# Four experts to a block in the last expert loads, and the modulation computed in three groups

## What is computed

```
mod = silu(c) @ w_ada + b_ada            # 1024 -> 6144, and w_ada_f: 1024 -> 2048
sh1, sc1, ga1, sh2, sc2, ga2 = split(mod);   shf, scf = split(silu(c) @ w_ada_f + b_ada_f)
u  = rmsnorm(h, g1) * (1 + sc1) + sh1
h += ga1 * mixer(u)                      # gated conv + gated linear attention, then w_out
u2 = rmsnorm(h, g2) * (1 + sc2) + sh2
h += ga2 * moe(u2)                       # 32 experts (1024 -> 512 -> 1024), 2 of 32 per token
h  = rmsnorm(h, g_final) * (1 + scf) + shf
out = second_block(h)                    # attention, pooling, state-space mixer, w_o, then a feed-forward with w_up, w_down
```

## Time and profile before

| | us |
|---|---|
| median of 3 runs | 1471.61 (1470.12 to 1472.62) |
| the profiled execution | 1468.99 |
| its span | 1467.2 |

### The profile page before, as it was taken

How to read it: one execution, slowest core, us unless ns; L and a number is a source line. 1 busy time by engine, 2 the same in 40 slices (tenths; PEclk the granted TensorE clock), 3 DMA queues, 4 the chain that set the end, 5 groups by cost and what they waited for, 6 DMA issues and landing times.

```text
span 1467.2 us, 20287 instructions
## 1 busy us (share of the span) xinstructions
PE 1226.6 (84%) x8730; PEld 969.2 (66%) x8730; DVE 672.8 (46%) x1103; ACT 456.0 (31%) x651; POOL 1.9 (0%) x15
## 2 busy tenths in 40 slices
PE   6989989998956657566675689999998989899998
PEld 4779887796423223132231389899997979899986
DVE  2647996553200000000000355356656777668974
ACT  1533333533000000000000343334545553554453
POOL 0000000000000000000000000000000000000000
PEclk8899999999979788798788789899998989999999
DMA  9785641996999999999999566343543335345552
GB/s 333 276 299 191 222 144 42 361 337 240 415 419 419 420 419 421 420 419 420 420 420 419 206 195 190 125 125 113 166 152 122 116 115 174 110 162 174 200 201 87
DMA packets 166151, 374.48 MB, mean 255 GB/s; under 512 B 5782, under 2 KB 118824, under 8 KB 141352
## 3 DMA queue, kind: packets, MB, share of 16 engines
q1 hardware_dynamic: 165888, 369.55, 67.8%
q0 software_dynamic: 144, 3.54, 0.7%
q10 hardware_dynamic: 24, 0.03, 0.0%
HBM read 372.02 MB, written 4.62 MB: 257 GB/s over the span
## 4 chain that ended last, share of the span: by engine, by line
PE 57%; DMA 22%; DVE 11%; SPq 5%; ACT 4%; issue 3%; DVEq 0%; ACTq 0%
PE bank L565 31%; DMA arena<-in_w 11%; DMA above<-in_w 8%; SPq L2485 4%; PE bank L1160 4%; DVE arena L1191 4%; PE bank L847 4%; DVE fine L1183 3%; ACT fine L1955 2%; DVE arena L1183 2%; PE bank L877 2%; PE bank L562 2%; PE bank L593 2%; ACT arena L1955 1%; DMA arena<-in_w_in 1%
## 5 line engine op out<-in xcount | busy, mean ns | idle before, releaser
L565 PE MATMUL bank<-fine 128*128 128x256 f32 x4656 | 587.5, 289 | 27.7 <-DVE fine L1183 17.0
L565 PEld LDWEIGHTS bank<-fine 128*128 128x128 f32 x4656 | 577.0, 196 | 37.2 <-issue 33.6
L1183 DVE TENSOR_TENSOR fine<-arena,fine 128x1024 fp32r<-128x1024 f32 (+2 forms) x263 | 300.4, 1167 | 179.7 <-ACT fine L1955 170.1
L1955 ACT ACTIVATE fine<-arena 128x1024 fp32r<-128x1024 f32 (+2 forms) x279 | 267.0, 984 | 181.6 <-PE bank L565 100.3
L1955 ACT ACTIVATE arena<-bank 128x256 f32<-128x256 f32 (+2 forms) x161 | 73.6, 484 | 566.7 <-PE bank L860 181.0
L847 PE MATMUL bank<-arena 128*32 128x512 f32 x640 | 126.1, 810 | 53.3 <-DMA arena<-in_w 34.0
L1183 DVE TENSOR_TENSOR arena<-arena,bank 128x512 f32<-128x512 f32 x8 | 8.4, 1054 | 290.7 <-PE bank L847 290.7
L847 PE MATMUL bank<-above,arena 128*32 128x512 f32 x384 | 78.9, 747 | 54.7 <-issue 25.0
L1955 ACT ACTIVATE arena<-arena 128x512 f32<-128x512 f32 (+6 forms) x94 | 63.2, 703 | 153.2 <-DVE arena L1183 62.0
L1191 DVE SCALAR_TENSOR_TENSOR arena<-arena 128x256 f32<-128x256 f32 (+3 forms) x262 | 107.6, 481 | 1.1 <-ACT arena L1955 0.8
L847 PEld LDWEIGHTS bank<-arena 128*32 128x32 f32 x640 | 31.3, 142 | 110.5 <-issue 110.4
(11 more groups left out here) (162 smaller groups left out, 775.0 us busy)
## 6 DMA issues: line engine op xcount, KB each, us to landing
arena<-in_w SPq DMA_DIRECT2D x120, 1024.0 KB, 26.9
above<-in_w SPq DMA_DIRECT2D x72, 1024.0 KB, 26.5
arena<-in_w_in SPq DMA_DIRECT2D x62, 1024.0 KB, 5.5
arena<-in_w_ada SPq DMA_DIRECT2D x24, 1024.0 KB, 8.9
arena<-in_ffn_w_up SPq DMA_DIRECT2D x22, 1024.0 KB, 5.1
arena<-in_ffn_w_down SPq DMA_DIRECT2D x11, 1024.0 KB, 5.0
arena<-in_w_ada_f SPq DMA_DIRECT2D x8, 1024.0 KB, 12.7
arena<-in_w_gla_o SPq DMA_DIRECT2D x4, 1024.0 KB, 12.1
```

What stands on the lines that cost most here:

```text
L565: ins = e.matmul(o, w[:, k, j * P:j * P + P], x[:, kt, :], start=start, stop=stop, skip_group_check=True)
L1183: return e.tensor_tensor(o, a, b, f)
L1955: return e.activation(o, i, f, bias=bias, scale=scale)
```

## The change

1. **Modulation in three groups**, `ADA = (0..3, 4..9, 10..15)`. All chunks of a group accumulate in bank 7: chunk i of a group puts its sums in row i of each 32-row tile, because the weight is now a window of a zeroed buffer `cz` in which only column 5 holds silu(c). One copy (`rows_ada(g)`), 4 products (`ada_to_mod(g)`, against 4, 6 or 6 columns of `sel`) and one `mod_of(g)` serve a whole group. 16 copies become 3, 64 turning products 12; the sums stay as many.
2. **Order.** Chunks 0 to 3 are loaded into eight separate buffers, without a wait. Chunks 10 and 11 move into level 4 of the mixer, 12 and 13 take the places of 10 and 11, and 14 and 15 those of 12 and 13. Nothing of the modulation is left behind the mixer's last product but the group's turn in quad 0.
3. **First piece.** `make_first` takes the products with the high input part k-tile by k-tile as ACT delivers them, for both halves, and those with the low part last. This holds for the first piece of q, of q2 and of up. For q, ACT and DVE also interleave the halves of the first weight piece with the input tiles.
4. **Two deeper flushes.** PE makes two more half pieces (`flush(1)`) ahead of its wait for the first decay factors and ahead of the wait for `decay_v["kd"]`.
5. **Last four blocks of the experts** (quad 7, blocks 8 to 11) hold one k-tile of all four experts instead of two of two; each is four DMAs of 512 KB instead of two of 1024 KB, in runs of 4 KB instead of 8 KB. PE takes each block by itself, with 8 products, in place of 16 for two blocks.

```diff
-        ada_slots = [flat(gates)[:, 0:SLOT], flat(gates)[:, SLOT:2 * SLOT], flat(St)[:, 0:SLOT], arena[:, q_at:q_at + SLOT]]
+        ada_slots = [flat(gates)[:, 0:SLOT], flat(gates)[:, SLOT:2 * SLOT], flat(St)[:, 0:SLOT], arena[:, q_at:q_at + SLOT],
+                     flat(v), scr[:, 0:SLOT], scr[:, SLOT:2 * SLOT], arena[:, q_at - SLOT:q_at],
+                     arena[:, early_at + SLOT:early_at + 2 * SLOT]]
...
             if f < 8:
-                return f % 4, ada_slots[f % 4], f - 4 if f >= 4 else None
+                return f, ada_slots[f], None
...
+            def make_first(p, half, bank):
+                name, ph = FACTOR[p.name], int(p.n >= PIECES1)
+                def products(kt, x, both, start=False, stop=False):
+                    parts = [shaped(w[:, 0:4 * p.width], 4, p.width) for w in w_parts[ph][(2 * p.n + kt // 4) % NU]]
+                    for j in range(p.width // P):
+                        for i, w in enumerate(parts[:1 + both]):
+                            ins = e.matmul(bank[:, j * 256:j * 256 + 256], w[:, kt % 4, j * P:j * P + P], x[ph][:, kt, :],
+                                           start=start and i + j == 0, stop=stop, skip_group_check=True)
+                    return ins
+                for kt in range(4 * half, 4 * half + 4):
+                    e.wait_ge(*x_hi_a[name, "tile", kt])
+                    products(kt, x_hi, True, start=kt == 0)
+                if half:
+                    for kt in range(KT):
+                        e.wait_ge(*x_lo_v[name, "tile", kt])
+                        ins = products(kt, x_lo, False, stop=kt == KT - 1)
+                        if kt % 4 == 3:
+                            ins.then_inc(*products_of.up((p.n, kt // 4)))
...
-                        ins = e.matmul(bank[32 * k:32 * k + 32, :], cact[:, kt:kt + 1].to_broadcast([P, 32]), slot[:, k, :],
-                                       start=f % 2 == 0, stop=f % 2 == 1, skip_group_check=True)
+                        ins = e.matmul(banks[7][32 * k:32 * k + 32, :], cz[:, kt, 5 - i:37 - i], slot[:, k, :],
+                                       start=f == 2 * ADA[g][0], stop=f == 2 * ADA[g][-1] + 1, skip_group_check=True)
...
+                    if li == 0:
+                        flush(1)
                     e.wait_ge(*decay_v["k", li])
...
-                if li < 4:
-                    ada_to_mod(6 + li)
+                if li == 3:
+                    ada_to_mod(1)
+                if li == 4:
+                    ada_sums(10)
                 for name in fill[done:done + LEVEL_PIECES[li]]:
                     advance(name, 1)
                 done += LEVEL_PIECES[li]
+                if li == 4:
+                    ada_sums(11)
                 if li == STATES_AT:
                     ke3 = shaped(ke, 4, 256)
+                    flush(1)
                     e.wait_ge(*decay_v["kd"])
...
-            ada_sums(10)
+            ada_sums(12)
             advance("gla_o", 2)
-            ada_sums(11)
-            ada_to_mod(10)
+            ada_sums(13)
             advance("gla_o", 2)
             flush()
-            ada_sums(12)
-            ada_to_mod(11)
+            ada_sums(14)
             advance("w_out", 2)
-            ada_sums(13)
-            ada_to_mod(12)
+            ada_sums(15)
             advance("w_out", 2)
             flush()
             norm(1)
-            ada_sums(14)
-            ada_to_mod(13)
-            ada_sums(15)
...
+                if quad == 7:
+                    for k in range(4):
+                        s, _, n = wide_of(quad, 8 + k)
+                        slot = shaped(wides[s], 4, 1024)
+                        e.wait_ge(*wide_in[s][n])
+                        for c in range(2):
+                            for x in range(4):
+                                ins = e.matmul(ob[c][32 * x:32 * x + 32, :], hidT[:, i, k, 32 * x:32 * x + 32],
+                                               slot[:, x, 512 * c:512 * c + 512], start=k == 0, stop=k == 3, skip_group_check=True)
+                        ins.then_inc(*down_made.up((quad, k)))
...
+            scale(0)
+            scale(1)
+            low_half()
+            scale(2)
+            scale(3)
+            low_half()
+            scale(4)
+            scale(5)
+            for k in range(4):
+                rest(k)
+            scale(6)
+            scale(7)
+            for k in range(4, KT):
+                rest(k)
...
+                if quad == 7 and i >= 8:
+                    for x in range(4):
+                        e.dma_start(shaped(wides[s], 4, 1024)[:, x, :], w2v[quad, :, x, i - 8, :]).then_inc(*wide_in[s].up(n, 16))
+                    return
...
-            load("gates", 8)
+            load("gates", 2)
             ada(10)
+            load("gates", 2)
+            ada(11)
+            load("gates", 4)
+            ada(12)
             load("pw", 2)
```

202 lines of the change are left out of this document (99 added, 103 removed).

## The result

| | before | after |
|---|---|---|
| median | 1470.86 (1469.76 to 1472.62) | 1444.75 (1444.07 to 1449.60, 4 runs) |
| the profiled execution | 1468.99 | 1444.07 |
| its span | 1467.2 | 1442.2 |

The same kernel measured once more, on another chip beside nine runs of before, gave 1447.95 against 1471.70, ratio 0.9854 [0.9833, 0.9876]; that time lies in the range. Between its two profiled executions the gain is 24.9 us (1468.99 to 1444.07), and this is the number that the rows can account for. Each kernel has one profiled execution, so a row that depends on the granted clock can differ in the next one; where a second profile tells, it is named.

What follows compares the result with a forecast made beforehand. Bound: PE, DVE and loads in turns through the first mixer, DMA over the experts, then PE. 15.4 + 2 - 0.3 + 2.2 = 19.3 us takes the profiled 1468.99 to 1449.7 and the median 1471.61 to 1452.3; range 1446 to 1461.

Steps and rivals of the forecast that it cites:

- part of it at half clock: At the start: PE's products of q's first piece run from 36.7 to about 47.0 us, partly at half clock.
- Part 1: The start: loads back to back and first input tile earlier, first piece ends sooner; gain 4.1 us, bounds 1.5 and 5.
- which takes about 2 back: Ahead of the experts: rows after some 5 us of PE idling run at half clock, taking back about 2 us.
- Part 5: Mixer's end to experts: PE reaches up products sooner, gain 2.2 us (0.5 to 4.2); block 8 issued 15.4 us earlier.
- Part 2: Up to the decay masks: fewer turns, idling filled, scores at full clock; PE 14.0 us ahead at about 105 us.
- Part 3: The mixer's seven levels: about 14.4 us where DVE becomes the bound, outputs 11 us earlier, bounds 7 and 14.
- rival (a): In the mixer: DVE eats PE's gain through waits for splits; total gain 9 to 14 us, about 1460; chance 0.22.
- Part 4: gla_o and w_out: the 7.53 us modulation wait stays, the turns behind it shrink; gain 2.2 us.
- Part 6: Behind the experts' last byte: 8 products instead of 16 gain 2 us (-1 to +4); shorter rows cost 0.3.
- Rival (d): Stream's end: each 512 KB DMA costs its own 4.5 us landing time; 33 us slower, 1504; chance 0.04.
- Part 7: Block two: first products of q2 and up no longer wait for the first low input tile; gain 2.2 us (1 to 3).
- Rival (b): Level 6 without idling (+3), router (+2) and last burst (+2) at full clock; gain 24 to 27, about 1446; chance 0.10.

Runs made afterwards that it cites:

- hold_scaled: The changed kernel with the loads of expert blocks 3 to 6 also waiting for the normalized input; one execution, 1458.13 us.
- before_again: The kernel before, unchanged, run once more for a second profile; 1470.13 us.
- no_level0_flush: The changed kernel without the flush of two half pieces ahead of the wait for the first decay factors; 1454.69 us, ratio 0.9890.
- first_u1_only: The changed kernel with the k-tile by k-tile order for q only, first pieces of q2 and up in the old order; 1449.47 us, ratio 0.9851.
- level0_flush_alone: The kernel before plus only the flush ahead of the wait for the first decay factors; 1461.19 us against 1472.16, ratio 0.9929.
- no_kd_flush: The changed kernel without the deeper flush ahead of the wait for the turned keys; 1448.52 us, ratio 0.9842.
- warm: kd_flush2 plus products of constant ones, into a bank nobody reads, where PE otherwise waits; 1437.70 us, ratio 0.9773.
- kd_flush2: The changed kernel with one more half piece, instead of two, ahead of the wait for the turned keys; 1445.85 us, ratio 0.9829; measured again 1447.17, ratio 0.9847.
- late_14_15: The changed kernel with loads, sums and copy of chunks 14 and 15 back behind the mixer's last product; 1450.05 us, ratio 0.9865.
- old_blocks: The changed kernel with the last four expert blocks as in the kernel before; 1448.78 us, ratio 0.9857.
- after_again: The changed kernel, unaltered, measured once more on another chip; 1447.95 us, ratio 0.9854.

## Why the prediction was right or wrong, point by point

The time fell below the range, and the step that failed is this: the sum priced PE's half clock behind an idle time with fixed amounts ("part of it at half clock" in Part 1, "which takes about 2 back" in Part 5, nothing in block two), and gave it no term in the range at the start or in block two. The runs show that the clock's return is not fixed: scores(0) at 99.11 to 106.69 us with the same code, and 24.5 to 27.5 us from norm(1) to the first up products. The direction and the mechanism of most parts were right; the sum was 5.6 us short between the profiled executions (24.9 for 19.3). Of this 4.1 us stand by the first up products, 0.6 from there to the send, 1.1 behind it (0.2 us is rounding and what lies around the span).

**Part 1** (4.1 forecast, 5.9 found): the gain of the first input tile came as worked out (33.78 for "near 35"). The step that failed is "part of it at half clock": in this execution the clock came back at 39 us. In hold_scaled, with the same code, L673 and the following 32 products took 4.2 us longer. Before's first profile had a late start too: in before_again the first piece ended at 48.8 (51.1), against which the gain is 3.6.

**Part 2** (scores(0) at 101.2 forecast, 99.11 found): idling gone, scores at 1.95 us, as forecast. The rest is Part 1's. That three other profiles have 101.2 to 101.4 is no confirmation, as they get there by a second loss of clock.

**Part 3** (14.4 where DVE bounds, 11 at the outputs; 16.9 and 14.6 found): of the 3.6 us too much at the outputs 2.1 stand at scores(0) already, so the mis-sized term is mainly the one at the start; from the taps on the loss is 2.3 us for 3.4 forecast. The wait in level 6 was foretold with its place and size (5 for 5.85). What the prediction undervalued is *why* the gain at level 0 lasts: it counted the two half pieces as 5.9 us of PE's work put into a gap, and had DVE "set the pace" from there without saying what releases DVE. The runs show that the second scores set DVE's pace: no_level0_flush loses 4.9 us there and still 5.9 at the outputs (against first_u1_only, whose start was as late), level0_flush_alone wins 7.5 and 7.4. For the same reason rival (a) had no ground: DVE full at 160 to 180 us means that it must be released earlier, not that it can't go earlier.

**The flush at the turned keys** was counted as a gain with a giving back in level 6. That is right in the net, and wrong in its reason: no_kd_flush shows idle time traded for idle time, and the clock as the difference.

**Part 4** (2.2 forecast, 0.9 found from the outputs to norm(1)): the modulation wait stayed, and took 8.94 us instead of 7.53, 1.4 us more, about what is missing. The second profile of before took 102.8 us on this way instead of 101.2, so a difference of 1 us here is not certain.

**Part 5** (2.2 forecast, bounds 0.5 and 4.2; 4.0 found, from 15.5 to 19.5): mis-sized by the clock. The step "which takes about 2 back" is true for the columns (5.14 us) but not for the gather, which ran at full clock here (3.81) and at 5.38 to 5.93 in warm and in both runs of kd_flush2. From norm(1) to the first up products the changed kernel and its close variants took 24.5 to 27.5 us and before and level0_flush_alone 28.6 to 30.9; the forecast says 26.4. The view of the release was right: the queue ran dry and block 8 followed the up products; late_14_15 shows that the loads' head start is worth nothing by itself.

**Part 6** (1.7 forecast, 2.4 shown by old_blocks): right, with 2.6 instead of 2 behind the last byte and 0.2 to 0.6 instead of 0.3 in the stream. Rival (d) has fallen. Its two numbers did not fit together either: it decides from 2.5 us a transfer on, so 3.2 us each would have made the kernel slower by some 12 us, and not 1468 us; the loss of 16 us counts the old transfers at the fit's price too.

**Part 7** (2.2 forecast, some 0.8 found): wrong. It was computed from one wait (851.03) as if PE's start decided. The start came (1.0 us at each place), but the first half's buffers come free later in the new order, and ACT's and DVE's splits, which wait for them, set the pace behind it: 0.8 us is left at q2, nothing at up. That send to end was 3.3 us shorter all the same in after is the clock.

**Rival (b)** (gain of 24 to 27 us, chance 0.10) is where the measured gain lies. Of its three reasons one came true in the profile, the gather at full clock; the idling in level 6 (5.85 us) and the half clock of the last burst (3.29 us) were there. The range's low end, 1446, cut off its upper half.

**The range.** It was built from unknown costs of the change alone. TensorE's clock after an idle time makes up to 7.6 us between executions of the same code at scores(0) and 3.6 us in block two (634.7 to 638.3 us over the profiles with the changed order there, warm apart), and no term had it in these two places; only the router had some in its bounds and in rival (b). Half of the first, some 3.5 us more at either end, and both measurements would have lain inside.

**What stays open.** The three profiles with the old block two have 641 us behind the send and the eleven others 634.6 to 638.3, though first_u1_only's products there are in the old order. The change has 0.8 us of this by the rows; the rest is where the clock falls, and that differs between after and after_again, one kernel. One or two profiles for each kernel don't tell why the three fell alike: by chance, or because the work before the waits comes at other times in the old order. Nor was it tried whether more products in the remaining waits (ahead of the gather, at 88 us) bring the rest.

## What to carry to other kernels

Ask of each wait of PE which engine is released by what stands *behind* it. Work that has to be done anyway pays in such a gap as far as the result behind it then comes earlier to the engine that bounds: DVE's masks waited for the second scores, and so one such line brought 7 of the 25 us. Price a wait of PE as its length plus what the rows behind it lose at half clock, and try filling it with work that nobody needs: that alone gave another 9.5 us in the medians. Judge steps of 1 to 3 us by the distance between two marks of the same profile, not by the total, and look first how much that distance differs between executions of the same code (1 us in the stream of the experts, 3 us on the way to them), and whether both profiles came to the first mark with the same clock.

## What the runs showed of the hardware that I had not expected

- An idle time of 3.57 us ahead of the turned keys cost 6.0 us in the three groups behind it (13.1 for 7.1); one of 0.69 us there cost nothing (1.09 and 4.01 us behind it, kd_flush2). But one of 2.10 us ahead of the same 72 products was followed by full clock in four profiles (8.9 us, as in after) and by a stretch at half clock in six (10.4 us, as in warm and hold_scaled).
- The return to full clock after the start varies by some 10 us between executions of the same code (39 to 40 us in seven profiles, 48 to 49 in first_u1_only and hold_scaled), and with it, and with the loss behind 2.10 us, scores(0) by 7.6 us.
- Small products of constants keep the granted clock at 1.00 through the whole of a stretch that otherwise ran at 0.50 (25 to 35 us, warm and after).
- 16 DMAs of 512 KB in runs of 4 KB in a full queue ran at 408 for 422 GB/s; the time from issue to landing of a single one, 4.5 us, is not seen in it.
